# Mixer of a two-layer encoder on one core: head diagonals before exponentials, sines two steps ahead, one GELU product on ScalarE, output matrices loaded unpadded

## What is computed

```python
z = rmsnorm(x, g_mix[i]) @ w_in[i]
u, q, k, v = jnp.split(z, splits, axis=-1)
# (a) state-space heads: 32 groups of 16 channels, 64 complex states, two directions
lam_bar = jnp.exp(lam * step)
b_bar = ((lam_bar - 1.0) / lam)[:, :, None] * b
bu = jnp.einsum('blgh,gph->blgp', u_c, b_bar)
states = scan(a1*a2, a2*b1 + b2) over (lam_bar, bu)   # forward and reversed
y = u * d_skip + sum over directions of Re(C states)
y = gelu(y);  y = y * sigmoid(y @ w_glu + b_glu);  y_ssm = rmsnorm(y, g_out)
# (b) differential attention: 4 heads, two softmax maps each
attn = softmax(s1) - lam * softmax(s2);  y_att = rmsnorm(attn @ v, g_subln)
x = x + concat([y_ssm, y_att]) @ w_out[i]
```

## Time and profile before

| what | us |
|---|---|
| median of 3 runs | 1429.87 |
| the runs | 1426.37, 1430.4, 1429.87 |
| the profiled execution | 1424.49 |
| its span | 1422.7 |
| PE busy in the span | 1337.5 (94%) |
| DVE busy | 852.9 (60%) |
| ACT busy | 679.5 (48%) |
| POOL busy | 134.3 (9%) |

### The profile page before, as it was taken

One profiled execution on the slowest core, in us unless ns is written; L12 is line 12 of the kernel. 1 busy time (PEld: TensorE's weight loads), 2 busy tenths in 40 slices (PEclk: granted clock), 3 DMA queues, 4 the chain that ended last, 5 costly groups with the idle time before them and its releaser, 6 DMA issues.

```text
span 1422.7 us, 18990 instructions
## 1 busy us (share of the span) xinstructions
PE 1337.5 (94%) x7246; PEld 970.9 (68%) x7246; DVE 852.9 (60%) x1095; ACT 679.5 (48%) x991; POOL 134.3 (9%) x111
## 2 busy tenths in 40 slices
PE   6996889999899888999999999999999999999996
PEld 5865558888787654876667676766766666666663
DVE  6868654454397875665554756555655555665552
ACT  6358443434274763344444544454544444444442
POOL 0356100000006640000000000000000000000000
PEclk9898999999999999999999999999999999999999
DMA  8352335453643236699999999999999999999994
GB/s 339 96 219 80 124 131 194 178 177 118 257 143 119 68 119 261 253 421 387 409 420 421 421 421 421 410 420 422 420 421 421 410 420 421 421 421 421 420 422 179
DMA packets 66328, 435.57 MB, mean 306 GB/s; under 512 B 8192, under 2 KB 14720, under 8 KB 16576
## 3 DMA queue, kind: packets, MB, share of 16 engines
q1 hardware_dynamic: 64848, 429.60, 75.1%
q0 software_dynamic: 1392, 4.78, 0.9%
HBM read 429.11 MB, written 2.10 MB: 303 GB/s over the span
## 4 chain that ended last, share of the span: by engine, by line
PE 74%; DVE 9%; DMA 8%; ACT 5%; SPq 2%; issue 1%; ACTq 0%; DVEq 0%
PE ps L2249 19%; PE ps L2284 11%; PE ps L2235 9%; PE ps L2138 8%; DMA raw<-wmoe 6%; PE ps L2266 6%; PE ps L2117 4%; PE ps L1902 3%; PE ps L2043 2%; PE ps L2058 2%; DMA first_ring<-wmoe 2%; PE ps L2020 2%; SPq L567 2%; PE ps L1943 1%; PE ps L2031 1%
## 5 line engine op out<-in xcount | busy, mean ns | idle before, releaser
L2138 PE MATMUL ps<-wsplit,xh 128*128 128x512 f32 (+1 forms) x352 | 112.6, 391 | 4.9 <-DVE hv L1429 3.3
L1439 DVE TENSOR_TENSOR low_raw<-raw,last_uppers 128x2048 fp32r<-128x2048 f32 x39 | 89.1, 2289 | 39.1 <-ACT last_uppers L869 39.1
L1439 DVE TENSOR_TENSOR low_first<-first_ring,first_uppers 128x2048 fp32r<-128x2048 f32 x31 | 70.8, 2291 | 37.6 <-ACT first_uppers L869 37.5
L1902 PE MATMUL ps<-hT,mixw 128*128 128x256 f32 x384 | 90.4, 398 | 2.6 <-DMA mixw<-wmix 1.6
L2284 PE MATMUL ps<-raw,hn 128*64 128x256 f32 x784 | 92.4, 382 | 0.0
L1439 DVE TENSOR_TENSOR low_raw<-raw,first_uppers 128x2048 fp32r<-128x2048 f32 x31 | 70.8, 2289 | 32.2 <-ACT first_uppers L869 32.2
L1403 DVE TENSOR_TENSOR wsplit<-raw,wsplit 128x2048 fp32r<-128x2048 f32 x33 | 74.5, 2289 | 20.1 <-ACT wsplit L828 20.1
L1902 PEld LDWEIGHTS ps<-hT,mixw 128*128 128x128 f32 x384 | 76.2, 200 | 15.2 <-issue 2.2
L1707 DVE TENSOR_TENSOR hv<-hv,ps 128x256 f32<-128x256 f32 x56 | 23.6, 421 | 103.8 <-ACT hv L1028 103.8
L2284 PE MATMUL ps<-last_ring,hn 128*64 128x256 f32 x704 | 83.2, 382 | 0.0
L1028 ACT ACTIVATE hv<-ps 128x256 f32<-128x256 f32 x56 | 21.5, 384 | 127.5 <-PE ps L2249 127.5
(11 more groups left out here) (367 smaller groups left out, 2930.1 us busy)
## 6 DMA issues: line engine op xcount, KB each, us to landing
raw<-wmoe SPq DMA_DIRECT2D x148, 1024.0 KB, 22.4
first_ring<-wmoe SPq DMA_DIRECT2D x95, 1024.0 KB, 23.2
last_ring<-wmoe SPq DMA_DIRECT2D x91, 1024.0 KB, 23.4
raw<-wdense SPq DMA_DIRECT2D x33, 1024.0 KB, 5.0
mixw<-wmix SPq DMA_DIRECT2D x12, 2048.0 KB, 8.3
cyt<-bmat SPq DMA_DIRECT2D x2, 2048.0 KB, 12.1
cw<-cmat SPq DMA_DIRECT2D x2, 2048.0 KB, 18.3
qk<-wglu SPq DMA_DIRECT2D x2, 1024.0 KB, 4.9
```

What stands on the lines that cost most here:

```text
L1439: tt(lows[at], ring[at], uppers[k % UPPERS].bitcast(F32), ALU.subtract).then_inc(s["lo_done"], 1)
L1902: ins = mm(ps[:, bank(u), j * 256:j * 256 + 256], mixw[:, c % 2, f, n * P:(n + 1) * P], hT[:, f, :], start=(f == 0), stop=(f == KT - 1))
L2138: ins = mm(to, x2[:, fx, t * P:(t + 1) * P], of, start=(fx == 0 and i == 0), stop=(fx == KT - 1 and i == 2))
```

## The change

- **Order within a step.** ScalarE does `T_DIAG` before `T_EXP`. Head 0's diagonals, which had no wait for a `turn`, now wait for the unit `zqkv5`.
- **Sines two steps ahead.** `trig` becomes `sines` and `cosines` with `TRIGS` = 4 slots, and step `i` makes those of `i+2`. The first two are made ahead of the loop, the second of them behind a wait for `cw_ready`.
- **GELU.** ScalarE squares y, copies it, and turns the square into 1 + 0.044715 y² (a third operation, behind a wait for the square). VectorE's `gelu_in` is one product of that with y read from PSUM. TensorE's next use of the bank waits for this product (`gin`).
- **Output matrices.** C is loaded unpadded (512 KB instead of 2048 KB for each layer) into two slots of `sines`. `fold_c` makes four products of 128x1024 and then four combinations of 64x1024 that write into `cw`, whose zeros GpSimd sets by a memset of 128x4096 at the head of each layer, in layer 1 once the dense part's last matmul is done.
- **Small constants.** Most rows of `small` move into the last slot of `sines` (`row`); the two that stay alive are in `kept`.

```diff
@@ loads and GpSimd @@
-                sp.dma_start(cw[:], cmat[l]).then_inc(s["in_c"], 16)
+                sp.dma_start(sines[:, 1:3], cmat[l]).then_inc(s["in_c"], 16)
...
             for l in range(DEPTH):
+                if l:
+                    pool.wait_ge(s["piece_done"], 3 * NC_D)
+                nc.gpsimd.memset(cw[:], 0.0).then_inc(s["cw_zero"], 1)
@@ trigs @@
-                if n >= 3:
-                    act.wait_ge(s["products"], n - 2)
+                if n >= TRIGS:
+                    act.wait_ge(s["products"], n - TRIGS + 1)
@@ take_y @@
                 act.wait_ge(s["c_done"], GP * l + 4 * (ft + 1))
+                chain[0] += 1
+                nc.scalar.activation(th[:, ft], y_sum, ACT.Square).then_inc(s["act_chain"], 1)
                 nc.scalar.activation(yt[:, ft], y_sum, ACT.Copy)
-                nc.scalar.activation(th[:, ft], y_sum, ACT.Square).then_inc(s["y_taken"], 1)
+                act.wait_ge(s["act_chain"], chain[0])
+                nc.scalar.activation(th[:, ft], th[:, ft], ACT.Copy, bias=1.0, scale=0.044715).then_inc(s["y_taken"], 1)
@@ diagonals @@
-                    if h:
-                        full(unit(l, f"turn{h - 1}"))
+                    full(unit(l, f"turn{h - 1}" if h else "zqkv5"))
@@ ScalarE's steps @@
                 nearest(l, 2)
                 trigs(l, 0)
+                act.wait_ge(s["cw_ready"], l + 1)
+                trigs(l, 1)
                 for i in range(STEPS):
-                    if i + 1 < GP:
-                        trigs(l, i + 1)
+                    if i + 2 < GP:
+                        trigs(l, i + 2)
...
-                    for at in (T_EXP, T_DIAG, T_TURN, T_OUT):
+                    for at in (T_DIAG, T_EXP, T_TURN, T_OUT):
@@ fold_c @@
-                c = [cw[:, r].rearrange("p i (j n) -> p (i j) n", j=2) for r in range(2)]
+                def c(r):
+                    return csrc[:, r].rearrange("p (i a) n -> p i a n", a=1).to_broadcast([P, ST, 2, GROUP])
                 dve.wait_ge(s["lamb_ready"], l + 1)
                 dve.wait_ge(s["in_c"], 16 * (l + 1))
-                tt(ctmp[:, 0], c[0], f(1), ALU.mult)
-                link(tt(ctmp[:, 1], c[1], f(1), ALU.mult))
-                tt(c[0], c[0], f(0), ALU.mult)
-                link(tt(c[1], c[1], f(0), ALU.mult))
-                tt(c[0], c[0], ctmp[:, 1], ALU.subtract)
-                stt(c[1], c[1], -1.0, ctmp[:, 0], ALU.mult, ALU.subtract).then_inc(s["cw_ready"], 1)
+                for k in range(2):
+                    for r in range(2):
+                        ins = tt(ctmp[:, 2 * k + r], c(r), f(k), ALU.mult)
+                link(ins)
+                dve.wait_ge(s["cw_zero"], l + 1)
+                for g in range(2):
+                    at = slice(STATE * g, STATE * (g + 1))
+                    to = cw[at].rearrange("p r i (j g n) -> p r i j g n", j=2, g=2)[:, :, :, :, g, :]
+                    tt(to[:, 0], ctmp[at, 0], ctmp[at, 3], ALU.subtract)
+                    ins = stt(to[:, 1], ctmp[at, 1], -1.0, ctmp[at, 2], ALU.mult, ALU.subtract)
+                ins.then_inc(s["cw_ready"], 1)
@@ gelu_in @@
-                link(stt(th[:, ft], th[:, ft], 0.044715, yt[:, ft], ALU.mult, ALU.mult))
-                tt(th[:, ft], th[:, ft], yt[:, ft], ALU.add).then_inc(s["gin"], 1)
+                tt(th[:, ft], th[:, ft], y_sum, ALU.mult).then_inc(s["gin"], 1)
@@ TensorE, outputs @@
-                    pe.wait_ge(s["y_taken"], FT * l + ft)
+                    pe.wait_ge(s["gin"], FT * l + ft)
```

More of the change, by code:

```diff
@@ L325, in encoder @@
         late = sb("late", [P, 5, SEQ])
-        trig = sb("trig", [P, 3, 3, SEQ])
+        sines = sb("sines", [P, TRIGS, 2, SEQ])
+        cosines = sb("cosines", [P, TRIGS, SEQ])
         ush = sb("ush", [P, PAIRS, NCH + 1])
         usw = sb("usw", [P, PAIRS, NCH])
-        small = sb("small", [P, 20, ST])
+        kept = sb("kept", [P, 2, ST])
         fold = sb("fold", [P, 2, 2 * ST])
@@ L462, in at_least, with row @@
                 eng.wait_ge(s[what], n)
+        passing = sines[:, 3].rearrange("p d (r n) -> p (d r) n", n=ST)
+        turn_rate, decay_rate = kept[:, 0], kept[:, 1]
+        csrc = sines[:, 1:3].rearrange("p b d (i n) -> p b (d i) n", n=GROUP)
+        def row(r, n=1):
+            at = r - 1 if r > 4 else r
+            return passing[:, at:at + n] if n > 1 else passing[:, at]
         def turn_part(i):
@@ L748, in phases @@
                         ins = nc.scalar.activation(turns_of(i)[:, d * NCH:(d + 1) * NCH], cst[:, C_T:C_T + NCH], ACT.Copy,
-                                                   scale=small[:, 4, 2 * i + d:2 * i + d + 1])
+                                                   scale=turn_rate[:, 2 * i + d:2 * i + d + 1])
                 chain[0] += 1
@@ L1227, in scalars @@
                 lre, lim = pr[:, Q_LRE:Q_LRE + ST], pr[:, Q_LIM:Q_LIM + ST]
[L1228 to L1229 removed]
+                tt(row(9), row(3), row(6), ALU.mult)
+                link(tt(row(10), row(3), row(5), ALU.mult))
                 def by(r):
[L1233 removed]
+                    return row(r).rearrange("p (i d) -> p i d", d=2)
                 def own(k):
@@ L1239, in other @@
                     return fold[:, k].rearrange("p (i x) -> p i x", x=4)[:, :, 1:3]
-                ts(sm[:, 17], sm[:, 9], -1.0, None, ALU.add)
-                tt(sm[:, 11], lre, lre, ALU.mult)
-                link(tt(sm[:, 12], lim, lim, ALU.mult))
-                link(tt(sm[:, 11], sm[:, 11], sm[:, 12], ALU.add))
-                nc.vector.reciprocal(sm[:, 11], sm[:, 11])
-                tt(sm[:, 12], sm[:, 17], lre, ALU.mult)
-                tt(sm[:, 13], sm[:, 10], lim, ALU.mult)
-                tt(sm[:, 18], sm[:, 10], lre, ALU.mult)
-                link(tt(sm[:, 19], sm[:, 17], lim, ALU.mult))
-                tt(sm[:, 12], sm[:, 12], sm[:, 13], ALU.add)
-                link(tt(sm[:, 18], sm[:, 18], sm[:, 19], ALU.subtract))
+                ts(row(14), row(9), -1.0, None, ALU.add)
+                tt(row(11), lre, lre, ALU.mult)
+                link(tt(row(12), lim, lim, ALU.mult))
+                link(tt(row(11), row(11), row(12), ALU.add))
+                nc.vector.reciprocal(row(11), row(11))
+                tt(row(12), row(14), lre, ALU.mult)
+                tt(row(13), row(10), lim, ALU.mult)
+                tt(row(15), row(10), lre, ALU.mult)
+                link(tt(row(16), row(14), lim, ALU.mult))
+                tt(row(12), row(12), row(13), ALU.add)
+                link(tt(row(15), row(15), row(16), ALU.subtract))
                 tt(own(0), by(12), by(11), ALU.mult)
-                link(tt(own(1), by(18), by(11), ALU.mult))
+                link(tt(own(1), by(15), by(11), ALU.mult))
                 tt(by(12), by(9), own(0), ALU.mult)
                 tt(by(13), by(10), own(1), ALU.mult)
-                tt(by(18), by(9), own(1), ALU.mult)
-                link(tt(by(19), by(10), own(0), ALU.mult))
+                tt(by(15), by(9), own(1), ALU.mult)
+                link(tt(by(16), by(10), own(0), ALU.mult))
                 tt(other(0), by(12), by(13), ALU.subtract)
-                link(tt(other(1), by(18), by(19), ALU.add))
+                link(tt(other(1), by(15), by(16), ALU.add))
             def turn_b(l):
@@ L1268, in lam @@
                 def lam(r, d):
-                    return (small[:, r].rearrange("p (k a d h) -> p k a d h", a=2, d=2, h=1)[:, :, :, d, :]
+                    return (row(r).rearrange("p (k a d h) -> p k a d h", a=2, d=2, h=1)[:, :, :, d, :]
                             .to_broadcast([P, PAIRS, 2, 32]))
@@ L1354, in scan @@
                 for d in range(2):
-                    decay = small[:, 16, 2 * i + d:2 * i + d + 1].to_broadcast([P, NCH])
+                    decay = decay_rate[:, 2 * i + d:2 * i + d + 1].to_broadcast([P, NCH])
                     for r in range(2):
```

61 lines of the change are left out of this document (29 added, 32 removed).

## The result

The changed kernel took 1410.76 us, the median of three executions (1405.29 to 1415.03), against 1429.87 before: a ratio of 0.9867 [0.983, 0.9904], 19.1 us. Faster was right; the amount was not. The profiled execution took 1415.03 (span 1413.2), the longest of the three, while the profiled one of before, at 1424.49, was shorter than all three timed beside it. Between these two the gain is 9.46 us, the sum almost to the hundredth.

What follows compares the result with a forecast made beforehand. It took TensorE to bound most of each mixer, and ScalarE and VectorE taking turns the middle part. 5.6 + 4.5 + 1.0 + 0.8 - 2.5 = 9.4 us off 1429.87 gave 1420.5, range 1411 to 1427.

Steps and rivals of the forecast that it cites:

- the sum: All terms of the forecast over both layers added up: 9.4 us won, chance 0.45.
- Attention schedule: Middle part of each mixer: diagonals first and sines two ahead end the waits, 5.6 us won in layer 0, 4.5 in layer 1.
- GELU: Two VectorE operations become one, ahead of a rotation that waits for nobody, so off the path: 0.
- Loads: 1.5 MB less loaded for each layer, with nothing in the trace waiting for it: 0.
- The memset: GpSimd's zeroing blocks VectorE at the head of layer 1: 4.5 us long, 2.5 us lost; 0 in layer 0.
- fold_c: Shorter fold removes TensorE's idle time ahead of local: 1.0 us won in layer 0, 0.8 in layer 1.
- Clock: Rival: layer 0's local stage keeps TensorE's full clock, 6.5 us more won, 1414.0; chance 0.17.
- The base: Gain set against the median 1429.87, as the profiled execution at 1424.49 ran 5.4 us under it.
- a gain in a mixer is passed on whole: Behind each mixer nothing depends on absolute time, so time won in either mixer shortens the kernel by as much.
- the ring of GpSimd: Rival: GpSimd's two steps and TensorE's outputs wait for each other, 2.4 us late in each layer, 1425.3; chance 0.08.
- the memset was short: Against the rival of a 10.2 us memset, costing 9.0 in layer 1 and perhaps 1.7 in layer 0, 1428.7; chance 0.08.
- the turns: Rival: ScalarE still waits for scores or a turn in the mixers, 2 us in each layer, 1424.5; chance 0.15.

Runs made afterwards that it cites:

- exp_first: Changed kernel with the next head's exponentials ahead of the diagonals again, sines still two steps ahead: 1414.94 us, ratio 0.9921.
- one_ahead: Changed kernel with the sines made one step ahead again, diagonals still first: 1421.66 us, ratio 0.9979.
- old_gelu: Changed kernel with GELU's start as before, two ScalarE and two VectorE operations for each half: 1410.75 us, ratio 0.9882.
- fold_only: Kernel before with only the compact load of the output matrices, the memset and the new fold: 1419.86 us, ratio 0.9937.
- before_again: Kernel before, unchanged, run and profiled once more: 1430.38 us.
- fed_all: Changed kernel with layer 1's memset earlier and filler matmuls ahead of local, first atn and output matmuls in each layer: 1413.8 us, ratio 0.9893.
- fed_sized: Changed kernel with layer 1's memset earlier, nine fillers ahead of the first atn and eight ahead of the output matmuls: 1407.23 us, ratio 0.9829.

## Why the prediction was wrong, by its own steps

- **Attention schedule, 5.6 and 4.5 us: right within 0.4 and 0.7 us.** Measured 6.0 and 5.2 between the first two profiles. The path of ScalarE up to the second tanh was 26.3 us for 26.44, VectorE's tail 8.1 for 8.25. exp_first and one_ahead show that neither half of the edit gives it alone, as the sum had assumed.
- **GELU, 0: wrong by a little.** old_gelu puts it at 1.2 us in layer 1, and at 0.5, within what varies, in layer 0. The step said that VectorE waits for nobody and so has time. In the profile after it waits for ScalarE's `take_y` twice in the stretch (0.93 and 0.25 us ahead of L1345), so both engines are on the path in turn, and two rows of 0.93 and 1.37 us, or 0.41 and 1.37, became one of 0.42.
- **Loads, 0.** No wait for `in_c` stands in the chains; nothing in the runs speaks against it, and none tested it by itself.
- **The memset, 2.5 us lost: right in kind, 1.9 in size.** It is the length of the memset that was over-rated (3.51 us, not 4.5). The rule of the Trainium skill cited for it (SBUF — State Buffer, "Who interferes with whom") agrees with the trace for the copy: the copy of two elements stood for 2.30 us beside the memset. Its other half, a memset beside an operation with both inputs in SBUF, no run shows: the two-input operation that kept 0.69 reads one input from PSUM.
- **fold_c, 1.0 and 0.8 us: this is the step that failed.** The profile showed 0.97 and 0.80 us of idle time ahead of `local`, and I took the idle time as all that its removal is worth. The same profile showed what mattered: 1.2 GHz for the stage right behind it, 6.5 us, in layer 0. I gave that 0.17 as the rival "Clock", for the reason that layer 1 had nearly the same idle time and kept its clock. The other profiles show why that was weak evidence: a wait of about 1 us can go either way (0.97 lost the clock, 0.80 and 1.07 kept it), longer ones (1.53, 2.05, 2.55) lost it each time, and the wait itself differs from execution to execution. Filling the idle time won 8 us, restoring it lost most of the gain, and fold_only alone won 9.7. The rule of the Trainium skill (TensorE: Matmul & The Clock Gate, "What's actually happening") pointed this way (the trace agrees: 0.50 behind the waits that lost it, 1.00 in all 25 places without one), and the rows of the profile did before it. The rival's 1414.0 counted layer 0 alone; layer 1 lost 7.9 in before_again. In layer 1 the idle time was also 2.55 in one profile, where 0.80 was read.
- **The base.** The profiled execution was set 5.4 us under the median without asking what made it so. No steady offset shows: the profile was one execution of a program whose clock differs by execution. Its loss in the `local` stage (6.5 us, 7.9 in before_again) was like that of the others, but it had less elsewhere: before_again took 2.9 and 1.9 us more in the two stages behind the mixers. Each stage as a mean over the profiles of the table gives 0.3 + 3.3 + 6.2 - 1.6 - 0.1 + 4.0 + 5.3 - 1.4 = 16.0 us for two of before against three of after, where the timed medians give 19 to 22; two and three profiles are too few for more. Between the first two profiles the step that a gain in a mixer is passed on whole failed too: 8.6 us were lost again behind the mixers.
- **What was left open.** Why the first `atn` pair falls to the low clock more often now (5.37 in three of six places, none of four before), part of the 1.6 + 1.4 us lost in the means, was not separated from chance. The output matmuls do not fall more often (8.83 in four of six places, three of four before). That it goes with the idle time ahead is shown by fed_all and fed_sized, one profile each.

The other rivals fell: the ring of GpSimd did not bind (34.7 and 34.4 us were measured where the sum without it had 35.1), the memset was short, and the turns did not stay.

## What to carry to other kernels

When a fully busy stage of TensorE shows a granted clock of 0.50 right behind an idle time, the idle time is priced at the clock of the stage behind it, not at its own length: here idle times of 0.97, 1.53, 2.05 and 2.55 us cost 6.5 to 8.1, while five of 0.33 to 1.07 cost no more than themselves. One profile tells in which stage that happened in one execution; look at a second profile, and at the mean clock of every timed execution, before a place is called safe. Two waits in one ring are worth little one by one, so try them together before either is given up.

## What the runs showed of the hardware

- The loss of clock differs from execution to execution of one program: the kernel before had it in layer 0 in one profile and in layer 1 in the next, with 61.95 and 63.39 us for a stage of 55.5, and mean clocks of its executions from 0.969 to 0.981. In part the idle time itself differs (0.97 us and none, 0.80 and 2.55); but behind the same 2.03 or 2.04 us the output matmuls lost the clock in 14 of 30 places.
- Matmuls whose results are thrown away can make a kernel faster: 21 of them won 8 us by the medians (ratio 0.9951 [0.9935, 0.9968]).
- A GpSimd memset of 4096 fp32 elements a lane took 3.51 to 3.54 us, 0.86 ns an element, about a third of the time per element of GpSimd's two-input operation (1.27 us for 512).
- A VectorE operation on two inputs in SBUF of 256 columns took 1.37 us while GpSimd was in its two-input operations, and 0.42 to 0.43 at its shortest (L1322 in the kernel before).
- A 128 x 128 fp32 matmul stands as two rows in the trace (x18 for nine in fed_sized), while a filler of 256 columns in the reduced fp32 type is one row: seven took 1.09 us.
